# Moving ScalarE's copy of the transposed probabilities, and TensorE's transposes, in the unit pipeline of an attention stage

## The reference

```
for each block of 128 queries (q_chunk, key_chunk: chunks of 64):
    sc = einsum('bqhcd,bkhcd->bhcqk', q_blk, k) * scale       # c = 0, 1: two score maps per head
    sc = where(key_chunk <= q_chunk, sc, min)
    p = softmax(sc, axis=-1)
    p_diff = p[:, :, 0] - lam * p[:, :, 1]
    o = einsum('bhqk,bkhe->bqhe', p_diff, v)
```

## Time and profile before

| | |
|---|---|
| median of 3 runs | 3220.45 us (3218.14 to 3227.24) |
| the profiled execution's own time | 3212.86 us |
| its span, first to last instruction | 3211.0 us |
| first scores matmul of the attention | 886.25 us |
| last VectorE copy of the attention starts | 1370.22 us |

### The profile page before, as it was taken

One profiled execution on the slowest core, in us unless ns is written; L12 is line 12 of the kernel. 1 busy time (PEld: TensorE's weight loads), 2 busy tenths in 40 slices (PEclk: granted clock), 3 DMA queues, 4 the chain that ended last, 5 costly groups with the idle time before them and its releaser, 6 DMA issues. The chain is left out here.

```text
span 3211.0 us, 66008 instructions
## 1 busy us (share of the span) xinstructions
PE 2963.3 (92%) x25434; PEld 1895.5 (59%) x25435; DVE 1552.7 (48%) x3592; ACT 1035.1 (32%) x2431; POOL 418.1 (13%) x620
## 2 busy tenths in 40 slices
PE   8999999999778888879999988999599999999999
PEld 6777777878545555578888874555233333333333
DVE  5676767777667677623333337786211111111111
ACT  3344334433367777722222222333100000000000
POOL 0000000000000000000000000000233333333333
PEclk9999999999989999989999999999699999999999
DMA  6121212111211000041111112334488888877663
GB/s 235 60 73 60 68 59 70 60 63 56 84 65 40 24 17 1 1 147 45 45 44 44 45 37 79 105 105 171 122 300 300 303 293 297 300 256 264 249 245 117
DMA packets 190196, 397.46 MB, mean 124 GB/s; under 512 B 16154, under 2 KB 76442, under 8 KB 188912
## 3 DMA queue, kind: packets, MB, share of 16 engines
q1 hardware_dynamic: 169440, 343.47, 30.4%
q0 software_dynamic: 20512, 50.54, 4.6%
HBM read 327.25 MB, written 80.32 MB: 127 GB/s over the span
## 5 line engine op out<-in xcount | busy, mean ns | idle before, releaser
L325 PE MATMUL pj_big<-pj_xnT,pj_w_in 128*128 128x256 f32 x2816 | 633.3, 381 | 4.3 <-ACT pj_ubuf L397 2.8
L325 PEld LDWEIGHTS pj_big<-pj_xnT,pj_w_in 128*128 128x128 f32 x2816 | 536.3, 191 | 85.1 <-ACT pj_ubuf L397 6.7
L1806 PE MATMUL ex_pgu<-keep_res,ex_xT 128*64 128x512 f32 x2560 | 569.3, 597 | 0.0
L1806 PEld LDWEIGHTS ex_pgu<-keep_res,ex_xT 128*64 128x64 f32 x2560 | 177.3, 137 | 335.2 <-issue 335.2
L1914 DVE TENSOR_TENSOR ex_hh<-ex_sg,ex_pgu 128x256 f32<-128x256 f32 x80 | 33.7, 421 | 584.3 <-ACT ex_sg L1879 584.3
L1824 PE MATMUL ex_py<-keep_res,ex_hT 128*64 128x512 f32 x1280 | 288.3, 592 | 1.0 <-DVE ex_yb L1922 1.0
L1325 PE MATMUL mg_po<-keep_res,mg_mix 128*128 128x512 f32 x512 | 232.4, 611 | 6.9 <-DVE mg_mix L1628 6.9
L737 ACT ACTIVATE at_e<-at_sc,at_nmx 128x512 f32<-128x512 f32 (+3 forms) x320 | 196.4, 620 | 111.7 <-DVE at_nmx L776 111.5
L776 DVE TENSOR_REDUCE at_nmx<-at_sc 128x2 f32<-128x1024 f32 (+3 forms) x160 | 170.2, 1063 | 102.8 <-PE at_sc L699 67.9
L1879 ACT ACTIVATE ex_sg<-ex_pgu 128x256 f32<-128x256 f32 x80 | 30.7, 383 | 581.6 <-PE ex_pgu L1806 581.6
L723 PE MATMUL at_op<-at_vh,at_pt 128*128 128x128 f32 x1088 | 161.5, 289 | 49.6 <-ACT at_pt L755 49.0
(11 more groups left out here) (293 smaller groups left out, 4761.1 us busy)
## 6 DMA issues: line engine op xcount, KB each, us to landing
keep_res<-in_w_exp_gate SPq DMA_DIRECT2D x32, 2048.0 KB
keep_res<-in_w_exp_up SPq DMA_DIRECT2D x32, 2048.0 KB
keep_res<-in_w_exp_down SPq DMA_DIRECT2D x32, 2048.0 KB, 8.8
chunks_s<-pj_st SPq DMA_DIRECT2D x32, 642.0 KB, 3.7
rw_raw<-chunks_s SPq DMA_DIRECT2D x32, 642.0 KB, 3.9
pj_xt<-in_x SPq DMA_DIRECT2D x20, 512.0 KB, 3.6
qk_s<-pj_qo SPq DMA_DIRECT2D x64, 128.0 KB, 1.9
mg_xin<-in_x SPq DMA_DIRECT2D x8, 1024.0 KB, 6.8
```

The costliest lines, as they stand in the source:

```text
L325: ins = pe.matmul(out, lhs, rhs, start=(k == 0), stop=(k == KC - 1))
L1806: ins = pe.matmul(pgu[j * BT:(j + 1) * BT, :, :], lhs, wgu[x][:, k, :, j * HE:(j + 1) * HE], start=(k == 0), stop=(k == KC - 1))
```

## The change

Two things change in `attention_steps`. `turn` is put in the list ahead of `soft` and one step later (unit k-8 in step k), and `values` is put one step later too (unit k-9). The list is one step longer. Every buffer and every wait of the engines' code stays as it is; the counts that `turn` and `values` wait for go by unit and not by step.

```diff
-    for k in range(NU + LAG + 2):
+    for k in range(NU + LAG + 3):
         if k < NU:
             steps += [("scores", k)]
         tile_ends = 1 <= k <= NU and (k == NU or UNITS[k][1] == 0)
         if tile_ends:
             steps += [("maxima", UNITS[k - 1][0])]
+        if 0 <= k - LAG - 2 < NU:
+            steps += [("turn", k - LAG - 2)]
         if k < NU:
             steps += [("soft", k)]
...
         if 0 <= k - LAG < NU:
             steps += [("combine", k - LAG)]
-        if 0 <= k - LAG - 1 < NU:
-            steps += [("turn", k - LAG - 1)]
-        if 0 <= k - LAG - 2 < NU:
-            u = k - LAG - 2
+        if 0 <= k - LAG - 3 < NU:
+            u = k - LAG - 3
             t, s = UNITS[u]
             steps += [("values", u)] + ([("out", t)] if u == last_unit(t) else [])
```

## The result

The changed kernel takes 3139.3 us (median of 4 runs, 3136.9 to 3142.8), against 3220.5 for the one before: a ratio of 0.9748, 95% interval 0.9733 to 0.9763. The profiled executions took 3212.86 and 3137.76 us.

What follows compares the result with a forecast made beforehand. The prediction took a loop through ScalarE's copy and the product to bound the attention; heads going from 118 to 103.3 us over 3.8 heads, less 1.5 at the end, gain 54.4 us, giving 3166 us, range 3143 to 3200.

Steps and rivals of the forecast that it cites:

- The loop: Attention: scores, maxima, exponentials, scaling, copy, product, 3.20 us a step; cut, the product's 12.6 us wait a head goes.
- What each engine has to do: Work in one attention head by starts of neighbouring instructions: TensorE 92.7 us, ScalarE 90.6, VectorE 86.7.
- The sum a head: One attention head: 96.6 us lower bound plus 6.7 us loss, 103.3 us, instead of 118 before.
- regions: A head's tiles of one to four units, each group's deciding engine charged: 11.7, 18.6, 27.6, 38.7 us; sum 96.6.
- lateness: VectorE's maxima late by 0.24 to 0.45 us at tile ends; 0.45 charged at 12 longer tiles' ends, 5.4 us a head.
- the 1.3 us of slack: Room in the remaining scores-maxima-exponentials loop (3.78 against 5.08 us), charged once a head as used up where VectorE decides.
- 3.8 heads of gain: From first transposes at about 905 us to 1353: 3.8 x (118 - 103.3) = 55.9 us gained, 54.4 after the end.
- TensorE's clock: Attention's granted clock 0.95 and 0.99; no gain taken, though by the skill's rule some 7 us could return, giving 3159.
- Nothing is lost in coupling: Rival: a head takes 96.6 us without coupling loss, gaining 79.9 us, time 3141 us; chance 0.10.
- VectorE's pace at tile ends: Rival: each tile end costs VectorE 3.32 us against TensorE's 2.54, unabsorbed; gain 26.7 us, time 3194; chance 0.17.
- The case of no gain: Rival: the wait only moves, before the next scores or the copy; within 10 us of the median, 3215; chance 0.06.
- The slower kernel: Rival: the copy holds up ScalarE at 16 tile ends a head, 4.32 us steps; 12 us slower, 3233; chance 0.05.

Runs made afterwards that it cites:

- the two half changes: Against the kernel before: only the copy moved ahead of the exponentials, 3156.3 us; only transposes and product a step later, copy still behind the exponentials, 3214.1 us.
- The load on the kernel before: Kernel before with two unused VectorE copies (0.41 us together) added at the ends of the 48 tiles of more than one unit: 3235.3 us, ratio 1.0049.
- the last kernel: Changed kernel with scaling on GpSimd, finished tiles' copy out on ScalarE, and the sign factor in GpSimd's scaling (the faster version): 3117.1 us, ratio 0.9671.
- lighter long tiles' ends: Changed kernel without VectorE's reciprocal and sign operations at the 48 tiles of more than one unit, results not normalised: 3127.4 us, stretch 388.8 us.

## Why the prediction was right in kind and wrong in size

**The loop.** Right. The product waited behind the copy behind the exponentials; of 12.6 us a head nothing is left, and the two half changes show that it is this loop (61 us by cutting it, 5 by the other part alone). The load on the kernel before adds that VectorE's tile ends were paid in that loop too, in part.

**The transposes' wait for `pd`, 5.3 us a head.** Right that it goes. Alone it is worth 5 us in all, since the loop takes most of it back; beside the cut loop its removal is worth 21 us, since without it that wait would be 11.5 us.

**What each engine has to do.** TensorE's 92.7 us by starts: measured 92.8 busy, and 92.3 a head in the last kernel, where little else is in the way. ScalarE's 90.6: 91.0. VectorE's 86.7: 84.5. These held.

**The sum a head, 96.6 + 6.7 = 103.3 us.** This is the step that failed: 6.7 us of loss from coupling was too much, and the 96.6 under it a little too much as well. Measured are 97.6 on average over the first three heads, and 98.2 over the second and third, in which the pipeline is full; the first, 96.5, is under the 97 that the forecast named as a sign of being wrong. The last VectorE copy starts at 1290.0 us and not at 1316. From one first correction to the fifth, ninth, thirteenth tile's and the next head's lie 5, 9, 13 and 13 steps. In these the charges, regions and lateness, come to 15.2, 22.7, 32.2 and 33.3 us. That is worked out from the forecast's rates: 2.93 us a unit for tiles of one unit, 2.33, 2.30 and 2.42 for the longer ones, 0.45 at each long tile's end and the 1.3 us. Measured, on average over the first three heads, are 11.97, 22.38, 31.41 and 31.88. The forecast is 0.3 and 0.8 us too high in the middle, 1.4 in the last quarter, and 3.2 in the first (2.5 against the 12.71 of the full heads; the first head's, 10.48 before and after, runs while the pipeline fills). The quarters of the third head:

```profile
1086.00:1098.80 12.80, 11.24 (x85) 8.06 (x82) 11.97 (x41) 11.39 (x35) 0.00 (x0) 1.00 0.04 17
1098.80:1120.90 22.10, 19.93 (x138) 13.67 (x136) 18.86 (x53) 19.70 (x60) 0.00 (x0) 1.00 0.18 49
1120.90:1152.00 31.10, 30.20 (x204) 20.43 (x202) 27.06 (x60) 29.75 (x84) 0.00 (x0) 1.00 0.01 2
1152.00:1183.90 31.90, 31.33 (x218) 22.09 (x218) 26.50 (x59) 30.01 (x84) 0.00 (x0) 1.00 0.01 1
```

In the first quarter VectorE is busy 11.97 of 12.80 us: it does decide there, as forecast. But I had charged four copies out there, though a copy out stands nine steps behind its last unit, so that most of them fall into other steps, and on top the 1.3 us of slack as a loss, where slack is what keeps a loss away. Even the regions alone, without any loss, give 13.45 us there, more than the 12.71 measured. In the last quarter TensorE is busy 31.33 of 31.90 us, which looks as if it filled that quarter. It does not: with lighter long tiles' ends the same quarter takes 30.9 us, with TensorE's work unchanged:

```profile
1145.20:1176.10 30.90, 30.86 (x217) 21.90 (x217) 25.34 (x51) 30.26 (x84) 0.00 (x0) 1.00 0.00 1
```

So about 1.0 us of VectorE's lateness was paid there, of 1.35 charged, and the region itself (31.97 by the rates) was charged at least 1.1 too high. Over a whole head the same kernel gives an estimate of both parts: 4.8 us less of VectorE's work at the 12 long ends took 3.2 us off a head (12.7 / 4). The lateness that the forecast put at 6.7 us is then worth some 3.2, all of it at the long ends and nothing for the 1.3 us of slack, and the regions some 95.0 instead of 96.6. VectorE's lateness is real, as the runs that lengthen and shorten it show, but it was mis-sized. I take it that VectorE's excess by region and its lateness by tile end are in part one quantity, counted twice, and that a delay of one engine is paid only where the one that decides there waits for it; that is argued and not measured by itself. By the rows, the measured head is TensorE's 92.8 us busy and 5.0 of waiting for the exponentials.

**3.8 heads of gain.** By the measured heads, 3.8 x (118 - 98.2) - 1.4 is 74 us, and 82.5 were seen. The first three heads gained 19.8, 20.3 and 21.1 us, and the fourth with the end 21.3. So the rest is partly my 118, where the heads measure 119 (3.4 us), and that four heads gained, not 3.8 (some 4 us). The end is the last part: from the last scores to the last VectorE copy it was forecast 1.4 us longer, and it is 0.8 shorter (16.8 to 16.0), though one more unit stands there.

**TensorE's clock.** In the window behind the first transposes the granted clock was 0.95 and is now 1.00. With what the Trainium skill says (Perfetto Trace Analysis, Matmul Optimizations) the direction agrees, but the first head gained no more than the second, whose clock was 0.99 and is 0.98: no gain from it can be told apart there. At the end it can. The same matmuls behind the last scores, before and after:

```profile
1358.60:1362.80 4.20, 4.13 (x21) 3.84 (x22) 2.85 (x8) 2.92 (x6) 0.00 (x0) 0.59 0.01 4
1279.90:1282.60 2.70, 2.56 (x21) 2.37 (x22) 2.47 (x7) 2.30 (x5) 0.00 (x0) 1.00 0.02 6
```

In both TensorE had just waited over a us for the copy (1.26 and 1.36), but only before was the granted clock then at the lower level. That cost 1.5 us, about what the added unit was to cost, so the end's coming out short is luck.

**The rivals.** "Nothing is lost in coupling" gave 3141 us and came nearest in time, but not in reason: ScalarE waits 6.1 and TensorE 5.0 us a head, and its 96.6 us a head were not reached. With the measured 98.2 in its own sum it would have said 3147; that it is near is partly luck. VectorE's pace at tile ends is in the stretch to 0.7 to 0.9 of each added or removed microsecond, and yet cost less than the forecast. The case of no gain needed the freed time to be lost before the next scores; TensorE's waits there are 5.0 us a head, of 17.9 freed. The slower kernel needed TensorE never to be ahead. It is, by a unit, in the timeline above.

## What to carry to other kernels

An in-order engine that stands in a loop can often be taken out of it by moving a ready instruction ahead of one that waits: look for the copy whose operand has been there for a step. When the loop is cut, sum up each engine's work by starts of neighbouring instructions, take the largest for each stretch, and then do not add a second loss for the engine that lags without asking whether the engine that decides would wait for it. An engine's busy time is no floor either: TensorE's 31.33 us in a quarter fell to 30.86 when only VectorE's work was cut. Where three engines are within a tenth of each other (92.8, 91.0 and 84.5 us here), adding a little work at one place at a time tells more than busy shares do.

## What was not expected of the hardware

GpSimd's scaling of 128x512 (tensor_scalar, SBUF to SBUF) took a median of 1.56 us where ScalarE took 0.71, and that was fast enough behind a pipeline of 2.4 us steps:

```profile
L758 POOL TENSOR_SCALAR at_tt<-at_e,at_cf x160: 602/1562/1987, 890.6 to 1274.5; 128x512 f32<-128x512 f32 x112, 128x128 f32<-128x128 f32 x16, 128x256 f32<-128x256 f32 x16, 128x384 f32<-128x384 f32 x16
L802 DVE SCALAR_TENSOR_TENSOR at_pd<-at_e,at_cf,at_tt x160: 340/742/1175, 902.8 to 1276.1; 128x512 f32<-128x512 f32 x112, 128x128 f32<-128x128 f32 x16, 128x256 f32<-128x256 f32 x16, 128x384 f32<-128x384 f32 x16
```

VectorE's combine beside it keeps its median of 0.74 us, and its longest went from 0.75 to 1.18. The Trainium skill (SBUF — State Buffer, SBUF: two separate sides) says that a VectorE operation with two SBUF inputs and a GpSimd operation that reads SBUF shut each other out for a whole instruction. The trace bears this out only in part. Of the 160 combines 51 lie wholly within the recorded time of a scaling; 40 of them keep their usual time to within 0.04 us, like this one, and no scaling beside them is longer:

```profile
907.54 1.56 POOL L758 TENSOR_SCALAR at_tt<-at_e,at_cf 128x512 f32<-128x512 f32 x1 [1.42 <-DVE at_pd L802]
908.16 0.74 DVE L802 SCALAR_TENSOR_TENSOR at_pd<-at_e,at_cf,at_tt 128x512 f32<-128x512 f32 x1
```

The 11 that are longer, by 0.20 to 0.43 us, all began at most 0.28 us after the scaling did. So what shuts the combine out here is the first 0.4 to 0.5 us of a scaling that lasts 1.24 or 1.56, by records that are rough for GpSimd.

With a second factor (`sign`) the same GpSimd operation took 0.80 us on average for 128x512, against 1.57 with one: the rows are with the faster version above. Why, no run here shows.
